# Hybrid pool/mLSTM block on one core: the eight kept weight units of z are loaded raw and split on the chip in every block

## The chip, the cores and the metric

The kernel runs on one core of a Trainium2 chip. The metric is the device time of one execution in microseconds (us), the median of several. In this text TensorE is PE in the profile (PEld its weight loads), VectorE is DVE, ScalarE is ACT, GpSimd is POOL, and SyncE is SP. A row with a q behind the engine (ACTq, SPq) is the issue of a DMA from that engine's queue.

## The reference, cut to what matters

```python
h = rms_norm(x, norm_g) * (1.0 + scale) + shift          # scale, shift, gate from c
proj = h @ w_in                                          # 1024 -> 8 groups of 512 columns
u, z_pool, q, k, v, o, z_mlstm, gates = split(proj)
pool_out = causal_pool_mixer(u, w_pool, ls_pool) * silu(z_pool)
q, k = silu(causal_depthwise_conv(q and k, conv_w, conv_b))   # 4 taps
hm = mlstm_chunkwise(q, k, v, ig, lf)                    # chunks of 128 positions, 4 heads
mlstm_out = norm(hm) * mh_norm_g * sigmoid(o) * silu(z_mlstm)
x = x + gate * (concat(pool_out, mlstm_out) @ w_out)
return rms_norm(x, final_g)
```

x is 1 x 4096 x 1024 in float32. All of it is computed to float32 accuracy.

## The kernel before

**Split operands.** A float32 product is made as three passes: both operands are split into a high part (rounded to the matmul's format) and a low part (the rest), and PE adds high times high, low times high and high times low. For a weight this split costs two instructions on 128 x 512 values: an ACT copy that writes the high part, and a subtraction that writes the low part, on POOL or on DVE. In block 0 the kernel splits the weights as they come, and stores most of them split in a DRAM tensor (w_kept); later blocks load high and low parts together from there (512 KB a unit) and need no split.

**Blocks and order of work.** The 4096 tokens go through in 8 blocks of 512. On PE every block but the first runs in this order: v for four chunks; the eight q and k tiles (tile 0 to 7, 24 matmuls of 512 columns each); z and o; then for each of four chunks the scores, a u tile, a z_pool tile, numerators and state update; and last the output projection.

**z and o by seven products.** In the blocks after the first, z_mlstm and o (two 2x2 halves each) are made by seven products in place of eight, in the order of `PRODUCTS = (1, 2, 6, 5, 7, 3, 4)`. Each product reads 4 weight units, so there are 28 units u = 0 to 27, with 6 matmuls of 512 columns each. Products 1 and 2 (units 0 to 7) read columns of z in `w_in`, product 4 columns of o, and the others sums of weights that block 1 leaves in `s_kept`. Before the change units 0 to 7 come split from w_kept (`ZO_KEPT = 8`), and units 8 to 27 come raw (256 KB a unit): ACT makes the high part (`split_zo`, L1128), and the low part is made on DVE for the units in `ZO_DVE` (8, 11, 13, 16, 18, 21, 23, 26; L1879) and on POOL for the other twelve (`ZO_POOL`, L1562).

**Ring.** Weight units live in a ring of 8 slots. SP issues one queue of loads in order; each load first waits until PE has used the unit that was in the slot. Units 0 to 7 of z take the slots of the k tiles' half units. From unit 10 on a keys transfer stands between every two loads (`keep_keys`), which waits for DVE's transposes of k (L2026).

**Beside the k tiles.** For each q or k tile, ACT copies the sum out of PSUM twice (L1396 and, with scale and bias, L1397), DVE runs three taps of the convolution (L2110), ACT takes the tanh (L1407), and DVE multiplies (L2126 or L2131). The four steps of a tile follow one another. Behind tile 5 ACT also computes `inter_exponents` (L1270), behind tile 6 it issues two small DMAs (`keep_rows`, L1274 and L1276), and behind tile 7 begins `zo_late`: there ACT splits unit 8, empties product 1's sums (`zo_hold`, L1323), and goes on with unit 9. Every engine runs its own instructions strictly in order; PE waits for each unit's low part by itself.

In block 1 DVE also has the sums `s_kept` and, behind tiles 3 and 5, part of the low halves of the token sums (`low_t`, L1918).

Of the kernel before, what the change touches and what calls it, by code (L numbers as in the profile page):

```python
# [45 lines left out]
OFF_U, OFF_ZP, OFF_Q, OFF_K, OFF_V, OFF_O, OFF_ZM, OFF_G = (512 * i for i in range(8))  # L46
# [9 lines left out]
QK_END = V_UNITS + 16  # L56
ZO_UNITS = 28
# [13 lines left out]

PRODUCTS = (1, 2, 6, 5, 7, 3, 4)
ZO_ORDER = (0, 3, 2, 1)
ZO_KEPT = 8
ZO_RAW = ZO_UNITS - ZO_KEPT
ZO_DVE = [u for u in range(ZO_KEPT, ZO_UNITS) if u % 5 in (1, 3)]
ZO_POOL = [u for u in range(ZO_KEPT, ZO_UNITS) if u not in ZO_DVE]
SUM_LOADS = {7: 1, 13: 2, 17: 3}
SUM_STORES = {10: 0, 15: 1, 18: 2, 22: 3}
SUMS_KEPT = QK_END + ZO_KEPT - 1  # L80


C_NG, C_C, C_BA, C_CW, C_CB, C_LS, C_MG, C_END = 0, 8, 16, 40, 72, 80, 84, 88
# [62 lines left out]
def build(nc, x, c, norm_g, w_ada, b_ada, w_in, b_gates, conv_w, conv_b, w_pool, ls_pool, mh_norm_g,  # L146
# [6 lines left out]
    with ExitStack() as ctx:  # L153
# [27 lines left out]
        s_kept = nc.dram_tensor("s_kept", [4, P, 2, D], F32, kind="Internal").ap()  # L181
# [244 lines left out]
        def _(sp):  # L426
# [38 lines left out]
            def load_w(b, m):  # L465

                slot_free(b, m)
                s = slot(b, m)
                sp.dma_start(both(w_split[:, s, :], m).bitcast(F32), both(w_kept[kept_at(b, m)], m)).then_inc(w_loaded[s], 16)

            def load_zo(b, u):

                m = QK_END + u
                if u < ZO_KEPT:
                    load_w(b, m)
                    return
                slot_free(b, m)
                product, k = PRODUCTS[u // 4], u % 4
                src = {4: w_in_v[:, 4 + k, OFF_O:OFF_O + 512], 3: s_kept[k][:, 1, 512:1024], 5: s_kept[k][:, 1, 0:512],
                       6: s_kept[k][:, 0, 512:1024], 7: s_kept[k][:, 0, 0:512]}[product]  # L480
                sp.dma_start(w_raw[:, slot(b, m), 512:1024], src).then_inc(w_loaded[slot(b, m)], 16)

# [239 lines left out]
        def _(pe):  # L722
# [67 lines left out]
            def one_block(b, last_block, first=False):  # L790
# [5 lines left out]
                def w_wait(m):  # L796
                    if first and m in RAW_NO:
                        pe.wait_ge(w_lo_done, RAW_NO[m] + 1)
                    else:
                        pe.wait_ge(w_loaded[slot(b, m)], 16 * loads(b, m))  # L800
# [101 lines left out]
                def zo_product(product):  # L902

                    of_t = {4: 3, 5: 0, 6: 1, 7: 2}
                    dst = {1: zo_x, 2: zo_z, 3: zo_w, 4: zo_x, 5: zo_y, 6: zo_x, 7: zo_x}[product]
                    for k in range(4):
                        u = 4 * PRODUCTS.index(product) + k
                        if u < ZO_KEPT:
                            w_wait(QK_END + u)
                        elif u in ZO_DVE:  # L910
                            pe.wait_ge(zo_lo_dve, (b - 1) * len(ZO_DVE) + ZO_DVE.index(u) + 1)
                        else:
                            pe.wait_ge(zo_lo_pool, (b - 1) * len(ZO_POOL) + ZO_POOL.index(u) + 1)
                        s = slot(b, QK_END + u)
                        for j in range(2):
                            if product in of_t:
                                n = of_t[product]
                                st_hi, st_lo = t_split[:, n, 0, j, k, :], t_split[:, n, 1, j, k, :]
                            else:
                                kk, c = (k if product == 1 else 4 + k), (2 + j if product == 3 else j)  # L920
                                st_hi, st_lo = hT_hi[:, kk, chunk(c)], hT_lo[:, kk, chunk(c)]
                            last = split3(dst[j][:, :], st_hi, st_lo, w_hi[:, s, :], w_lo[:, s, :],
                                          k == 0 and product not in (4, 6, 7), k == 3, product in (4, 6, 7))
                            if k == 3:
                                last.then_inc(zo_full, 1)
                            elif j == 1:
                                last.then_inc(zo_used, 1)
# [186 lines left out]
        def _(act):  # L1114
            def split_w(m):

                if m not in RAW_NO:
                    return
                act.wait_ge(w_loaded[slot(0, m)], 16 * loads(0, m))
                hi, lo = halves(m)  # L1120
                act.activation(w_split[:, slot(0, m), hi], w_raw[:, slot(0, m), lo], ACT.Copy).then_inc(w_hi_done, 1)

            def split_zo(b, u):

                m = QK_END + u
                s = slot(b, m)
                act.wait_ge(w_loaded[s], 16 * loads(b, m))
                act.activation(w_split[:, s, 0:512], w_raw[:, s, 512:1024], ACT.Copy).then_inc(zo_hi_done, 1)  # L1128
# [100 lines left out]
            def one_block(b, last_block, first=False):  # L1229
# [99 lines left out]
                def zo_late():  # L1329

                    early, after = [oz[:, j, :] for j in range(2)], [oz[:, 2 + j, :] for j in range(2)]
                    split_zo(b, 8)
                    zo_hold(1, early)
                    exponents()
                    for u in range(9, 14):
# [43 lines left out]
                for t in range(16 if first else 8):  # L1379
# [28 lines left out]
                    else:  # L1408
# [1013 lines left out]
```

## Time and profile before

| | us |
|---|---|
| median of 3 runs | 1754.94 |
| lowest and highest run | 1753.93, 1758.83 |
| profiled execution, its own time | 1755.37 |
| profiled execution, span from first to last instruction | 1753.5 |
| PE busy (share of the span) | 1718.7 (98%) |
| DVE busy | 1262.0 (72%) |
| ACT busy | 709.6 (40%) |
| POOL busy | 308.5 (18%) |

The granted TensorE clock is 0.995 of full speed over the span. A timeline row gives the start, the duration, engine, line and operation, the tiles written and read, and in brackets how long the engine sat idle before it and what ended that. Where the instruction count is more than one (x3), the duration is that of all of them together. Pipelined instructions overlap a little: a following ACT operation starts about 0.1 us before the one ahead has ended by its row.

### The profile page before, as it was taken

Reading aid. Unit: us, or ns where it says so; the run is one execution under the profiler, and the core shown is the slowest. Engines: PE = TensorE matmul, PEld = TensorE weight load, DVE = VectorE, ACT = ScalarE, POOL = GpSimd, SP = SyncE. Lnnn points to the kernel's source line nnn. Section 1 sums busy time; section 2 is a strip of 40 time slices with the busy share of each in tenths; the row PEclk is TensorE's granted clock in tenths of the full one; section 3 lists DMA queues with packets and bytes.
Section 4 is the critical chain, followed back from the end, with each engine's and each line's share of the span. In section 5 each row is a group of like instructions: output and inputs, shape, how many; then the busy total and the mean of one; then the engine's idle time right before and its main releaser. Section 6 shows DMA issues by size and latency. Waiting matters only on the chain.

```text
span 1753.5 us, 25355 instructions
## 1 busy us (share of the span) xinstructions
PE 1718.7 (98%) x8921; PEld 1472.6 (84%) x8921; DVE 1262.0 (72%) x2599; ACT 709.6 (40%) x1636; POOL 308.5 (18%) x265
## 2 busy tenths in 40 slices
PE   5999999999999999999999999999999999999998
PEld 5987879878898888988888888888889888898886
DVE  7785788767876677766876668866787658776683
ACT  4445343353433434334433434435343343433421
POOL 0022222030210303003030211303021030300300
PEclk9899999999999999999999999999999999999999
DMA  9989875989556984669737796468955698456852
GB/s 335 324 296 325 242 190 198 345 212 300 142 188 192 251 270 120 209 200 270 231 103 244 224 282 172 163 205 229 301 142 191 192 249 276 115 211 202 256 162 84
DMA packets 393554, 387.75 MB, mean 221 GB/s; under 512 B 258300, under 2 KB 283860, under 8 KB 392916
## 3 DMA queue, kind: packets, MB, share of 16 engines
q1 hardware_dynamic: 378196, 363.44, 67.9%
q10 hardware_dynamic: 15232, 22.69, 4.2%
q8 instruction: 71, 1.16, 0.3%
q14 instruction: 55, 0.45, 0.1%
HBM read 323.99 MB, written 62.06 MB: 220 GB/s over the span
## 4 chain that ended last, share of the span: by engine, by line
PE 86%; DVE 5%; DMA 4%; ACT 1%; issue 1%; SPq 1%; POOL 0%; ACTq 0%; POOLq 0%; DVEq 0%
PE ps_acc L725 19%; PE ps_acc L727 19%; PE ps_acc L726 18%; PE ps_num L725 4%; PE ps_num L727 4%; PE ps_num L726 4%; PE ps_kv L725 2%; PE ps_kv L726 2%; PE ps_kv L727 2%; PE ps_sco L1027 2%; PE ps_num L1046 1%; PE ps_kv L1052 1%; PE ps_num L1045 1%; PE ps_bro L725 1%; PE ps_bro L727 1%
## 5 line engine op out<-in xcount | busy, mean ns | idle before, releaser
L725 PE MATMUL ps_acc<-sb_hT_hi,sb_w_split 128*128 128x512 f32 x1024 | 406.0, 396 | 1.1 <-DVE sb_w_split L1857 1.0
L727 PE MATMUL ps_acc<-sb_hT_hi,sb_w_split 128*128 128x512 f32 x1024 | 399.5, 390 | 0.0
L726 PE MATMUL ps_acc<-sb_hT_lo,sb_w_split 128*128 128x512 f32 x1024 | 398.6, 389 | 0.0
L727 PEld LDWEIGHTS ps_acc<-sb_hT_hi,sb_w_split 128*128 128x128 f32 x1024 | 192.2, 188 | 41.3
L725 PEld LDWEIGHTS ps_acc<-sb_hT_hi,sb_w_split 128*128 128x128 f32 x1024 | 192.4, 188 | 40.6 <-issue 1.9
L726 PEld LDWEIGHTS ps_acc<-sb_hT_lo,sb_w_split 128*128 128x128 f32 x1024 | 192.6, 188 | 37.6
L1562 POOL TENSOR_TENSOR sb_w_split<-sb_w_raw,sb_w_split 128x512 fp32r<-128x512 f32 x84 | 115.1, 1377 | 565.3 <-ACT sb_w_split L1128 565.2
L1128 ACT ACTIVATE sb_w_split<-sb_w_raw 128x512 fp32r<-128x512 f32 x140 | 86.2, 631 | 80.6 <-DMA sb_w_raw<-s_kept 74.3
L2110 DVE SCALAR_TENSOR_TENSOR sb_acc_cv<-sb_shifted,sb_par,sb_acc_cv 128x512 f32<-128x512 f32 x96 | 73.7, 767 | 53.3 <-ACT sb_acc_cv L1397 50.4
L1879 DVE TENSOR_TENSOR sb_w_split<-sb_w_raw,sb_w_split 128x512 fp32r<-128x512 f32 x56 | 59.6, 1064 | 66.2 <-ACT sb_w_split L1128 65.9
L1573 POOL TENSOR_TENSOR sb_h_rs<-sb_h_var,sb_mhalf 128x4 f32<-128x4 f32 x32 | 32.3, 1010 | 401.4 <-DVE sb_h_var L2202 401.4
L725 PE MATMUL ps_acc<-sb_wo_hi,sb_mixm_hi 128*128 128x512 f32 x256 | 100.6, 393 | 1.3 <-DVE sb_silu_zp L2319 1.3
L725 PE MATMUL ps_acc<-sb_wo_hi,sb_mixp_hi 128*128 128x512 f32 x256 | 101.7, 397 | 0.0
L726 PE MATMUL ps_acc<-sb_wo_lo,sb_mixp_hi 128*128 128x512 f32 x256 | 100.2, 392 | 0.0
L727 PE MATMUL ps_acc<-sb_wo_hi,sb_mixp_lo 128*128 128x512 f32 x256 | 100.2, 391 | 0.0
L727 PE MATMUL ps_acc<-sb_wo_hi,sb_mixm_lo 128*128 128x512 f32 x256 | 99.8, 390 | 0.0
L726 PE MATMUL ps_acc<-sb_wo_lo,sb_mixm_hi 128*128 128x512 f32 x256 | 99.7, 389 | 0.0
L2110 DVE SCALAR_TENSOR_TENSOR sb_hm<-sb_shifted,sb_par,sb_hm 128x512 f32<-128x512 f32 x96 | 73.1, 762 | 25.1 <-ACT sb_hm L1397 21.1
L725 PE MATMUL ps_kv<-sb_w_split,sb_hT_hi 128*128 128x256 f32 x256 | 73.7, 288 | 5.6 <-DVE sb_hT_lo L1748 5.6
L726 PE MATMUL ps_kv<-sb_w_split,sb_hT_hi 128*128 128x256 f32 x256 | 73.0, 285 | 0.0
L727 PE MATMUL ps_kv<-sb_w_split,sb_hT_lo 128*128 128x256 f32 x256 | 72.7, 284 | 0.0
L1442 ACT ACTIVATE sb_tanh<-sb_hm 128x128 bf16<-128x128 f32 x128 | 38.0, 298 | 83.9 <-DVE sb_hm L2184 83.9
(293 smaller groups left out, 3929.7 us busy)
## 6 DMA issues: line engine op xcount, KB each, us to landing
sb_w_split<-w_kept SPq DMA_DIRECT2D x288, 512.0 KB, 4.8
sb_w_split<-w_kept SPq DMA_DIRECT2D x56, 520.0 KB, 4.6
sb_w_raw<-s_kept SPq DMA_DIRECT2D x112, 256.0 KB, 4.2
sb_w_raw<-w_in SPq DMA_DIRECT2D x76, 256.0 KB, 4.7
sb_x_res<-x SPq DMA_DIRECT2D x34, 512.0 KB, 4.7
w_kept<-sb_w_split SPq DMA_DIRECT2D x32, 512.0 KB, 6.3
out<-sb_qT SPq DMA_DIRECT2D x32, 512.0 KB, 2.9
sb_x_in<-x SPq DMA_DIRECT2D x112, 128.0 KB, 3.9
```

Source lines behind the costliest of these rows:

```text
L725: pe.matmul(dst, st_hi, mv_hi, start=start, stop=False, skip_group_check=resumed)
L726: pe.matmul(dst, st_hi, mv_lo, start=False, stop=False, skip_group_check=resumed)
L727: return pe.matmul(dst, st_lo, mv_hi, start=False, stop=stop, skip_group_check=resumed)
L1027: last = pe.matmul(sco[:, chunk(h)], kT[:, j, h, :], qT[:, h, chunk(j)], start=True, stop=True)
L1045: pe.matmul(dst, dmat[:, h, :], v[:, j, h, :], start=True, stop=False)
L1046: last = pe.matmul(dst, q_in[:, h, :], cmem[:, h, :], start=False, stop=True)
L1128: act.activation(w_split[:, s, 0:512], w_raw[:, s, 512:1024], ACT.Copy).then_inc(zo_hi_done, 1)
L1442: last = act.activation(junk[:, chunk(h)], hm[:, h, :], ACT.Square, accum_out=h_sq[:, h:h + 1])
L1562: nc.gpsimd.tensor_tensor(w_split[:, s, 512:1024], w_raw[:, s, 512:1024], w_split[:, s, 0:512].bitcast(F32), ALU.subtract).then_inc(zo_lo_ ...
L1573: nc.gpsimd.tensor_tensor(dst, src, mhalf[:, 0:n], ALU.pow).then_inc(done, 1)
L1879: V.tensor_tensor(w_split[:, s, 512:1024], w_raw[:, s, 512:1024], w_split[:, s, 0:512].bitcast(F32), ALU.subtract).then_inc(zo_lo_dve, 1)
L2110: ins = V.scalar_tensor_tensor(conv[t % 2], sh[:, HALO - 3 + n:HALO - 3 + n + BLK], tap[n], conv[t % 2], ALU.mult, ALU.add)
```

## The change

No unit of z and o is kept split any more: `ZO_KEPT` becomes 0, so that all 28 units are loaded raw in blocks 1 to 7, and block 0 does not store its eight units of z. ACT gets eight more splits in each of the blocks 1 to 7: units 0 and 1 behind the tanh of tile 5, units 2 and 3 behind that of tile 6, units 4 and 5 behind that of tile 7, and 6 and 7 at the head of `zo_late`. POOL gets their eight low halves (`ZO_POOL` has now 20 units); DVE's units stay the same.

```diff
-ZO_KEPT = 8
+ZO_KEPT = 0
 ZO_RAW = ZO_UNITS - ZO_KEPT
-ZO_DVE = [u for u in range(ZO_KEPT, ZO_UNITS) if u % 5 in (1, 3)]
+ZO_DVE = [u for u in range(8, ZO_UNITS) if u % 5 in (1, 3)]
 ZO_POOL = [u for u in range(ZO_KEPT, ZO_UNITS) if u not in ZO_DVE]
-SUMS_KEPT = QK_END + ZO_KEPT - 1
+SUMS_KEPT = QK_END + 7
...
             def load_zo(b, u):
 
                 m = QK_END + u
-                if u < ZO_KEPT:
-                    load_w(b, m)
-                    return
                 slot_free(b, m)
                 product, k = PRODUCTS[u // 4], u % 4
-                src = {4: w_in_v[:, 4 + k, OFF_O:OFF_O + 512], 3: s_kept[k][:, 1, 512:1024], 5: s_kept[k][:, 1, 0:512],
+                src = {1: w_in_v[:, k, OFF_ZM:OFF_ZM + 512], 2: w_in_v[:, 4 + k, OFF_ZM:OFF_ZM + 512],
+                       4: w_in_v[:, 4 + k, OFF_O:OFF_O + 512], 3: s_kept[k][:, 1, 512:1024], 5: s_kept[k][:, 1, 0:512],
...
-                        if u < ZO_KEPT:
-                            w_wait(QK_END + u)
-                        elif u in ZO_DVE:
+                        if u in ZO_DVE:
                             pe.wait_ge(zo_lo_dve, (b - 1) * len(ZO_DVE) + ZO_DVE.index(u) + 1)
...
-                    split_zo(b, 8)
+                    for u in range(6, 9):
+                        split_zo(b, u)
                     zo_hold(1, early)
...
+                    if not first and t >= 5:
+                        split_zo(b, 2 * (t - 5))
+                        split_zo(b, 2 * (t - 5) + 1)
                     if t == 5:
                         inter_exponents()
```

On ACT, these are the instructions of block 1 from just behind the tanh of tile 5 to `zo_late`'s exponents (rows of the changed kernel carry its own line numbers: L1393, L1394 and L1404 are what L1396, L1397 and L1407 were, L1124 is the split). Before:

```order
L1270 ACTIVATE sb_silu_zp<-sb_m_row,sb_mp_col 16x128
L1396 ACTIVATE sb_shifted<-ps_acc 128x512
L1397 ACTIVATE sb_acc_cv<-ps_acc,sb_par 128x512
L1407 ACTIVATE sb_tanh<-sb_acc_cv 128x512
L1274 DMA rows_kept<-sb_m_row 16x128
L1276 DMA rows_kept<-sb_silu_zp 16x128
L1396 ACTIVATE sb_shifted<-ps_acc 128x512
L1397 ACTIVATE sb_hm<-ps_acc,sb_par 128x512
L1407 ACTIVATE sb_tanh<-sb_hm 128x512
L1128 ACTIVATE sb_w_split<-sb_w_raw 128x512
L1323 ACTIVATE sb_oz<-ps_num 128x512 x2
L1288 ACTIVATE sb_expo<-sb_expo 128x48
```

With the change, the same place:

```order
L1124 ACTIVATE sb_w_split<-sb_w_raw 128x512 x2
L1266 ACTIVATE sb_silu_zp<-sb_m_row,sb_mp_col 16x128
L1393 ACTIVATE sb_shifted<-ps_acc 128x512
L1394 ACTIVATE sb_acc_cv<-ps_acc,sb_par 128x512
L1404 ACTIVATE sb_tanh<-sb_acc_cv 128x512
L1124 ACTIVATE sb_w_split<-sb_w_raw 128x512 x2
L1270 DMA rows_kept<-sb_m_row 16x128
L1272 DMA rows_kept<-sb_silu_zp 16x128
L1393 ACTIVATE sb_shifted<-ps_acc 128x512
L1394 ACTIVATE sb_hm<-ps_acc,sb_par 128x512
L1404 ACTIVATE sb_tanh<-sb_hm 128x512
L1124 ACTIVATE sb_w_split<-sb_w_raw 128x512 x5
```

Two splits now stand ahead of tile 6's copies, two ahead of the small DMAs and tile 7's copies, and five in place of one behind tile 7's tanh.

On POOL, this is where block 1 begins its work on z. Before, and then with the change:

```order
L1573 TENSOR_TENSOR sb_o_rs<-sb_o_var,sb_mhalf 128x1
L1562 TENSOR_TENSOR sb_w_split<-sb_w_raw,sb_w_split 128x512 x12
L1573 TENSOR_TENSOR sb_h_rs<-sb_h_var,sb_mhalf 128x4 x3
L1573 TENSOR_TENSOR sb_x_rs<-sb_x_var,sb_mhalf 128x4 x2
L1573 TENSOR_TENSOR sb_h_rs<-sb_h_var,sb_mhalf 128x4
```

```order
L1573 TENSOR_TENSOR sb_o_rs<-sb_o_var,sb_mhalf 128x1
L1562 TENSOR_TENSOR sb_w_split<-sb_w_raw,sb_w_split 128x512 x20
L1573 TENSOR_TENSOR sb_h_rs<-sb_h_var,sb_mhalf 128x4 x3
L1573 TENSOR_TENSOR sb_x_rs<-sb_x_var,sb_mhalf 128x4 x2
L1573 TENSOR_TENSOR sb_h_rs<-sb_h_var,sb_mhalf 128x4
```

Twelve low halves have become twenty in each block, with the eight new ones first. On SP's queue, block 2 loads its q, k and first z units. Before, and then with the change:

```order
L469 DMA sb_w_split<-w_kept 128x2x520 x3
L469 DMA sb_w_split<-w_kept 128x1024 x24
L481 DMA sb_w_raw<-s_kept 128x512 x2
L536 DMA keys_kept<-sb_hm 32x16x32
L481 DMA sb_w_raw<-s_kept 128x512
```

```order
L469 DMA sb_w_split<-w_kept 128x2x520 x3
L469 DMA sb_w_split<-w_kept 128x1024 x16
L479 DMA sb_w_raw<-w_in 128x512 x8
L479 DMA sb_w_raw<-s_kept 128x512 x2
L534 DMA keys_kept<-sb_hm 32x16x32
```

The eight loads stand at the same places of the queue, with half the bytes and another source.

## Rows read from the trace of the kernel before

**Rows 1.** Waits of PE from 300 us on, in total, times, longest.

```profile
PE ps_num L725 <- DVE sb_w_split L1879: 1.7, 1, 1.7
```

**Rows 2.** PE timeline: block 4, first matmuls of products 1 and 6.

```profile
982.08 0.39 PE L725 MATMUL ps_num<-sb_w_split,sb_hT_hi 128*128 128x512 f32 x1
...
992.96 0.39 PE L725 MATMUL ps_num<-sb_w_split,sb_t_split 128*128 128x512 f32 x1
```

**Rows 3.** ACT timeline, block 4, from tile 5's tanh to unit 9's split.

```profile
975.68 0.63 ACT L1407 ACTIVATE sb_tanh<-sb_hm 128x512 f32<-128x512 f32 x1 [3.14 <-DVE sb_hm L2110]
976.21 0.39 ACT L1270 ACTIVATE sb_silu_zp<-sb_m_row,sb_mp_col 16x128 f32<-16x128 f32 x1
...
977.21 0.77 ACT L1397 ACTIVATE sb_acc_cv<-ps_acc,sb_par 128x512 f32<-128x512 f32 x1
980.37 0.63 ACT L1407 ACTIVATE sb_tanh<-sb_acc_cv 128x512 f32<-128x512 f32 x1 [2.39 <-DVE sb_acc_cv L2110]
...
980.74 0.43 ACTq L1276 DMA_DIRECT2D rows_kept<-sb_silu_zp  x1
...
982.77 0.77 ACT L1397 ACTIVATE sb_hm<-ps_acc,sb_par 128x512 f32<-128x512 f32 x1
985.94 0.63 ACT L1407 ACTIVATE sb_tanh<-sb_hm 128x512 f32<-128x512 f32 x1 [2.40 <-DVE sb_hm L2110]
...
988.80 0.64 ACT L1128 ACTIVATE sb_w_split<-sb_w_raw 128x512 fp32r<-128x512 f32 x1
```

**Rows 4.** DVE timeline, block 4: tile 6's taps, unit 8's low half.

```profile
978.01 2.33 DVE L2110 SCALAR_TENSOR_TENSOR sb_acc_cv<-sb_shifted,sb_par,sb_acc_cv 128x512 f32<-128x512 f32 x3 [0.78 <-ACT sb_acc_cv L1397]
...
990.21 1.15 DVE L1879 TENSOR_TENSOR sb_w_split<-sb_w_raw,sb_w_split 128x512 fp32r<-128x512 f32 x1
```

**Rows 5.** POOL timeline, block 4: its first low half, unit 9.

```profile
989.51 1.29 POOL L1562 TENSOR_TENSOR sb_w_split<-sb_w_raw,sb_w_split 128x512 fp32r<-128x512 f32 x1 [69.99 <-ACT sb_w_split L1128]
```

**Rows 6.** POOL and DVE timelines, block 0, taps beside two low halves.

```profile
112.42 3.00 POOL L1556 TENSOR_TENSOR sb_w_split<-sb_w_raw,sb_w_split 128x512 fp32r<-128x512 f32 x2 [80.29 <-DVE sb_w_split L1857]
...
112.94 3.81 DVE L2110 SCALAR_TENSOR_TENSOR sb_acc_cv<-sb_shifted,sb_par,sb_acc_cv 128x512 f32<-128x512 f32 x3 [0.58 <-ACT sb_acc_cv L1397]
```

**Rows 7.** Block 1: ACT's three tanhs of tiles 5 to 7, DVE's token halves.

```profile
351.28 0.63 ACT L1407 ACTIVATE sb_tanh<-sb_hm 128x512 f32<-128x512 f32 x1 [4.67 <-DVE sb_hm L2110]
...
357.84 0.63 ACT L1407 ACTIVATE sb_tanh<-sb_acc_cv 128x512 f32<-128x512 f32 x1 [4.49 <-DVE sb_acc_cv L2110]
...
362.43 0.63 ACT L1407 ACTIVATE sb_tanh<-sb_hm 128x512 f32<-128x512 f32 x1 [2.39 <-DVE sb_hm L2110]
...
352.68 2.50 DVE L1918 TENSOR_TENSOR sb_t_split<-sb_t_raw,sb_t_split 128x512 fp32r<-128x512 f32 x4
```

**Rows 8.** PE timeline, block 1: first matmuls of products 1, 2 and 6.

```profile
354.26 0.39 PE L725 MATMUL ps_num<-sb_w_split,sb_hT_hi 128*128 128x512 f32 x1
...
360.13 0.47 PE L725 MATMUL ps_acc<-sb_w_split,sb_hT_hi 128*128 128x512 f32 x1 [0.27 <-issue]
...
367.49 0.47 PE L725 MATMUL ps_num<-sb_w_split,sb_t_split 128*128 128x512 f32 x1 [1.65 <-DVE sb_w_split L1879]
```

**Rows 9.** SP timeline, block 4: loads of units 4 to 7.

```profile
973.98 8.61 SPq L469 DMA_DIRECT2D sb_w_split<-w_kept  x4
```

**Rows 10.** The page's DMA issues: KB each, median us from issue to landing.

```profile
sb_w_split<-w_kept SPq DMA_DIRECT2D x288, 512.0 KB, 4.8
```

**Rows 11.** PE timeline, block 0, two matmuls behind an idle stretch.

```profile
254.21 0.49 PE L734 MATMUL ps_bro<-sb_x_sq,sb_same_row 128*128 128x4 f32 x2 [2.24 <-ACT sb_tanh L1149]
...
255.56 0.63 PE L727 MATMUL ps_acc<-sb_wo_hi,sb_mixp_lo 128*128 128x512 f32 x1
255.99 0.63 PE L725 MATMUL ps_acc<-sb_wo_hi,sb_mixp_hi 128*128 128x512 f32 x1
```

**Rows 12.** Busy time by window, with granted clock, DMA share and GB/s.

```profile
255.00:260.00 5.00, 5.00 (x17) 3.94 (x17) 2.16 (x6) 3.40 (x12) 4.22 (x4) 0.72 0.92 138
...
140.00:160.00 20.00, 19.26 (x101) 16.07 (x100) 12.52 (x15) 10.93 (x18) 7.64 (x6) 1.00 1.07 367
```

## The prediction, written before the changed kernel was timed

> **What bounds the kernel now.** I read the busy shares first (the table above): PE is busy for 98% of the span, so time can be lost or won only where PE stands. The view of waits says where: from 300 us on, PE waits once for more than 0.3 us, in block 1 [rows 1]. So blocks 2 to 7 are pure PE time, and anything that makes PE wait there adds to the end, once a block. The first matmul of product 1 in block 4 is at 982.08 and that of product 6, 48 matmuls later, at 992.96 [rows 2]: one matmul each 0.227 us, 1.36 us for a unit's six, 5.44 us for a product or a tile. So unit u is due at 982.08 + 1.36 u: unit 2 at 984.80, unit 4 at 987.52, unit 7 at 991.60. DMA is not what PE waits for in these blocks.
>
> The question is thus whether each of units 0 to 7 has its low part when PE gets there. The timeline of ACT in block 4 [rows 3] shows how far ACT's tile chain lies behind PE: tile 7's sums are ready at 982.08, but its tanh only starts at 985.94. The split of unit 4 now stands behind that tanh. I work through block 4 in order.
>
> **The loads: cost nothing.** SP issues the four loads of units 4 to 7 from 973.98 to 982.59 [rows 9], and such a load lands after 4.8 us [rows 10], so unit 4 is there at 979 and unit 7 at about 987, both ahead of their splits below. They have half the bytes now. If this cover went, ACT would stall in order, with all of its chain.
>
> **Two splits behind tile 5.** A 0.63 us activation gives way to the next after 0.53 us (975.68 to 976.21 [rows 3]). Two take 1.06, so `inter_exponents` starts at 977.27, and tile 6's copies 0.3 us later (its 0.39 less the same overlap of 0.1): L1396 at 977.56, L1397 0.49 later at 978.05 instead of 977.21. The taps started 0.80 behind L1397 (978.01 [rows 4]), so at best at 978.85. Meanwhile POOL starts 0.07 us behind a split's end (988.80 + 0.64 to 989.51 [rows 3, 5]): unit 0 from 976.91 to 978.20, unit 1 to 979.49, at 1.29 each.
>
> **POOL and the taps together.** The trace has one place where taps run beside two low halves: the three take 3.81 us instead of 2.33, the two low halves 3.00 instead of 2.58, and they alternate: the first tap waits for the first low half, holds the second up by 0.42, and taps two and three end 1.33 us behind POOL's end [rows 4, 6]. So a DVE operation with two SBUF inputs and such a POOL operation exclude each other. A third tap adds 0.79 (2.33 less one tap's 0.75, halved), so three taps that wait for the end of a low half end 2.12 us after it. Here: 979.49 + 2.12 = 981.6 and tanh 6 there, instead of 980.37, that is 1.2 late. Without the exclusion it would be 978.85 + 2.33 = 981.2. The Trainium skill (SBUF — State Buffer, section "SBUF: two separate sides") calls this pair of ports an exclusive lock, held for the whole instruction by whichever of the two engines starts first. The trace agrees for DVE, which waits out the low half, and differs for POOL, which is held for 0.42 us of a tap's 0.75; by the rule the unit held up at the end below would come 0.3 us later still, 2 us over the run.
>
> **Two splits behind tile 6.** Tanh 6 at 981.6, unit 2's split at 982.15, unit 3's at 982.7. The two small DMAs issue only when unit 3's split has been sent off: they end 0.79 after it (0.37 from tanh 6 to the start of the second, which takes 0.43 [rows 3]), and with 0.1 to spare tile 7's copies start at 983.6 and L1397 at 984.1, instead of 982.77. POOL: unit 2 from 982.85 to 984.15 (due 984.80, in time), unit 3 to 985.45 (due 986.16, in time). The taps could start at 984.9, wait for unit 3's low half, and end at 985.45 + 2.12 = 987.55: tanh 7 there instead of 985.94.
>
> **Behind tile 7: PE waits.** Unit 4's split runs from 988.1 to 988.7, its low half from 988.8 to 990.07. PE was due at 987.52, so it waits **2.55 us**. From there units come each 1.30 us from POOL and go each 1.36 us to PE. DVE's low half of unit 8 (990.21 before [rows 4], 1.6 later now) holds one of them up by 0.42: PE waits about **0.25 us** more, at unit 7. Unit 8 and all behind it are wanted 2.8 us later than before, while their loads are held by the key transposes, which move by only 1.6: no wait more. Sum: **2.8 us a block**, six blocks 2 to 7: 16.8.
>
> **Block 1** is worse, since its tile chain is later: product 1 starts at 354.26 [rows 8] but tanh 5, 6 and 7 are at 351.28, 357.84 and 362.43 [rows 7]. Unit 0's low half fits (352.5 to 353.8). Then POOL and DVE's four token halves (352.68, 2.50 us for four) get into each other: two low halves of 1.29 go between, so DVE is 2.2 us later and tanh 6 is at 360.0. Unit 2's low half then ends at 360.0 + 0.53 + 0.63 + 0.07 + 1.29 = 362.6, due 357.0: PE waits 5.6. Unit 3's ends at 363.9, tanh 7 follows 2.12 later at 366.0, and unit 4's low half ends 2.52 behind it at 368.5; PE, through with unit 3 at 365.3, waits 3.2. Before, product 2 started at 360.13: 8.4 later. Of this the old waits, 1.65 and 0.16 us ahead of units 8 and 10 (the first in [rows 8]), are absorbed, as those units are then long ready; 0.25 for unit 7 comes to it: 6.8.
>
> **TensorE's clock.** The trace shows what idling can cost: PE sat idle for 2.24 us, and then matmuls that take 0.39 us took 0.63, one each 0.43 us instead of 0.23 [rows 11], with a granted clock of 0.72 in that stretch [rows 12]; that is the lower of its two levels, 1.2 GHz, for some eight matmuls, and cost 8 x 0.20 = 1.6 us. Behind the idle 1.65 us in block 1 they had their usual pitch. My 2.55 us lie just above the idling that did it. So I count 1.6 us in four blocks of the six and nothing in the others (bounds 0 and 9.6), and 1 us in block 1: 7.4.
>
> **Block 0** loses eight stores of 512 KB between 119 and 135 us, where the DMA engines have no room (share 1.07 at 140 to 160 [rows 12]). PE idles 0.74 of the 20 us there, so the most that this can give is about 1; I take 0.5.
>
> Sum: 16.8 + 6.8 + 7.4 - 0.5 = 30.5. Added to the profiled execution's own time, 1755.37 (0.4 above the median of the runs), that is 1785.9: **1786 us**.
>
> **Bounds.** Low: no exclusion and no fall of the clock. Tanh 6 at 981.2, tile 7's L1397 at 983.7, tanh 7 at 986.8, unit 4 ready at 989.3: 1.8 a block, 10.8 for six; block 1 has then tanh 6 as before, at 357.84, and unit 4 ready 5.9 later than before, 4 net. 1755.4 + 14.8 = 1770. High: 3.3 a block (POOL held for each tap's whole 0.75), the clock low in each block, 10 for block 1 (6.8 and both its waits with the clock's 1.6): 6 x (3.3 + 1.6) + 10 = 39.4, 1795.
>
> **Rivals.** A: *POOL and DVE hardly meet and the clock holds*: 1770 to 1778. For it: small shifts decide whether a tap asks for the port during a low half. Against it: POOL's two low halves behind tiles 5 and 6 cover 2.6 us in which the taps fall due each time. B: *each stall drops the clock and the loss breeds more*: units 9 and 10 also come late because POOL has 8 more operations of 1.29 us (10.3 a block) at a pace that is PE's own. 1795 to 1805. Against it: POOL is busy for 18% of the span and sat idle before unit 9. C: *no change*: the splits fall into ACT's idle 2.39 us before each tanh, and PE is not touched. It needs unit 4 by 987.52, that is tanh 7 at 985.1 at the latest, when even before the change it was at 985.94. That holds it down. D, on the other side: *the relief of the DMA engines in block 0 decides*: PE is idle for 0.74 of 20 us there [rows 12], and for as much again in the windows around, 3 us at most; if all that goes and the z units are in time, 1752, and 1749 if the old waits of block 1 and its neighbours go too. It decides from the point where tanh 7 comes 0.8 us earlier than in the rows; nothing in the change brings that.
>
> **How the numbers follow.** Forecast (1778 to 1796) 0.62; A 0.15; B 0.11; between C and A (1761 to 1770) 0.05; C 0.04; D 0.03. The range from 1770 to 1797 takes in the forecast and A and leaves out less than 2 in 10. A measurement of this kernel can tell about 0.3% (5 us) from no change: faster 0.03, same 0.05, slower 0.92.
>
> **What the changed profile would show.** PE's first matmul of product 2 waits for POOL's low half, once in each of blocks 2 to 7, about 2.5 us; twice in block 1, 5.6 and 3.2. ACT's tanh 6 comes about 1.2 and tanh 7 about 1.6 us later against product 1's start. Taps that last over 2.33 us stand beside POOL's low halves. Behind some of the waits the matmuls take 0.63 us. I am wrong if no such wait is there, if it is for a DMA, or if time is lost in the out projection or at the u tiles, where I expect everything moved along together.

## The result, and the profile of the changed kernel

The changed kernel took **1787.03 us** (median of 4 runs, 1781.94 to 1788.87) against 1754.43 us for the kernel before in the same session (4 runs, 1753.54 to 1758.83): ratio 1.0176, 95% interval 1.0156 to 1.0197. The profiled execution took 1787.7 us, its span is 1785.9 us, 32.4 more than before.

I read the waits of PE from 300 us on first, since the one row of [rows 1] is what the kernel before had there. The columns are as there: total, times, longest.

```profile
PE ps_acc L723 <- POOL sb_w_split L1562: 18.9, 7, 2.8
PE ps_num L723 <- POOL sb_w_split L1562: 5.3, 1, 5.3
PE ps_bro L1005 <- DVE sb_m_row L2003: 1.5, 1, 1.5
```

The old wait is gone, and GpSimd's low halves are now what PE waits for, eight times. (The third row stands at 345.89, ahead of product 1 of block 1, and e5 below, which has none of the new work, waits 1.46 us there too.) The PE timeline says where: the first matmul of product 2, in block 1 at unit 2 and again at unit 4 (the first two rows), then once in each block. Three of the six blocks stand here, with the first matmul of product 1 of block 4 as the mark that answers to [rows 2].

```profile
359.77 0.80 PE L723 MATMUL ps_num<-sb_w_split,sb_hT_hi 128*128 128x512 f32 x1 [5.27 <-POOL sb_w_split L1562]
366.10 0.66 PE L723 MATMUL ps_acc<-sb_w_split,sb_hT_hi 128*128 128x512 f32 x1 [1.91 <-POOL sb_w_split L1562]
...
578.90 0.47 PE L723 MATMUL ps_acc<-sb_w_split,sb_hT_hi 128*128 128x512 f32 x1 [2.83 <-POOL sb_w_split L1562]
579.21 0.39 PE L724 MATMUL ps_acc<-sb_w_split,sb_hT_hi 128*128 128x512 f32 x1
...
995.85 0.39 PE L723 MATMUL ps_num<-sb_w_split,sb_hT_hi 128*128 128x512 f32 x1
...
1004.29 0.58 PE L723 MATMUL ps_acc<-sb_w_split,sb_hT_hi 128*128 128x512 f32 x1 [2.84 <-POOL sb_w_split L1562]
1004.67 0.63 PE L724 MATMUL ps_acc<-sb_w_split,sb_hT_hi 128*128 128x512 f32 x1
1005.10 0.63 PE L725 MATMUL ps_acc<-sb_w_split,sb_hT_lo 128*128 128x512 f32 x1
...
1217.13 0.47 PE L723 MATMUL ps_acc<-sb_w_split,sb_hT_hi 128*128 128x512 f32 x1 [2.83 <-POOL sb_w_split L1562]
```

Behind the wait at 578.90 the matmuls keep 0.39 us; behind that at 1004.29 they take 0.63, one each 0.43, as in [rows 11]. The windows (busy times as in [rows 12], then granted clock, DMA share, GB/s) show it for blocks 2, 3, 4 and 5: full clock in blocks 2 and 5, lowered in 3 and 4. By the rows of all six blocks the clock is low for 14 matmuls in blocks 3 and 6, for 8 in blocks 4 and 7.

```profile
578.00:582.00 4.00, 3.10 (x14) 2.59 (x15) 3.72 (x5) 3.39 (x8) 4.00 (x4) 1.00 0.59 142
790.00:794.00 4.00, 3.77 (x9) 3.06 (x10) 3.06 (x4) 2.43 (x6) 4.00 (x4) 0.50 0.71 155
1004.00:1008.00 4.00, 3.71 (x9) 2.94 (x10) 3.11 (x4) 3.12 (x7) 4.00 (x4) 0.57 0.73 174
1217.00:1221.00 4.00, 3.87 (x17) 3.23 (x18) 2.98 (x4) 2.97 (x7) 4.00 (x3) 1.00 0.81 181
```

Why POOL is late is seen in block 4. First ACT, which answers to [rows 3]; product 1 starts at 995.85 now, so tile 5's tanh stands 6.40 us ahead of it as before, tile 6's 0.46 ahead (before 1.71) and tile 7's 5.80 behind (before 3.86).

```profile
989.45 0.63 ACT L1404 ACTIVATE sb_tanh<-sb_hm 128x512 f32<-128x512 f32 x1 [3.14 <-DVE sb_hm L2110]
989.99 1.14 ACT L1124 ACTIVATE sb_w_split<-sb_w_raw 128x512 fp32r<-128x512 f32 x2
...
995.39 0.63 ACT L1404 ACTIVATE sb_tanh<-sb_acc_cv 128x512 f32<-128x512 f32 x1 [2.83 <-DVE sb_acc_cv L2110]
...
1001.65 0.63 ACT L1404 ACTIVATE sb_tanh<-sb_hm 128x512 f32<-128x512 f32 x1 [3.43 <-DVE sb_hm L2110]
1002.19 2.69 ACT L1124 ACTIVATE sb_w_split<-sb_w_raw 128x512 fp32r<-128x512 f32 x5
```

Then POOL and DVE in the same stretch (POOL's three rows first), which answer to [rows 4, 5].

```profile
990.69 2.55 POOL L1562 TENSOR_TENSOR sb_w_split<-sb_w_raw,sb_w_split 128x512 fp32r<-128x512 f32 x2 [57.31 <-ACT sb_w_split L1124]
996.62 2.54 POOL L1562 TENSOR_TENSOR sb_w_split<-sb_w_raw,sb_w_split 128x512 fp32r<-128x512 f32 x2 [3.39 <-ACT sb_w_split L1124]
1002.88 9.74 POOL L1562 TENSOR_TENSOR sb_w_split<-sb_w_raw,sb_w_split 128x512 fp32r<-128x512 f32 x7 [3.71 <-ACT sb_w_split L1124]
...
992.60 2.76 DVE L2110 SCALAR_TENSOR_TENSOR sb_acc_cv<-sb_shifted,sb_par,sb_acc_cv 128x512 f32<-128x512 f32 x3 [0.58 <-ACT sb_acc_cv L1394]
...
996.99 0.96 DVE L2014 COPY sb_m_prev<-sb_m_prev 128x4 f32<-128x4 f32 x1
997.98 1.20 DVE L2106 COPY sb_shifted<-sb_halo_qk 128x3 f32<-128x3 f32 x1
999.29 2.33 DVE L2110 SCALAR_TENSOR_TENSOR sb_hm<-sb_shifted,sb_par,sb_hm 128x512 f32<-128x512 f32 x3
```

For comparison, DVE at the same place in the kernel before, where POOL is idle and the taps wait for ACT's copy:

```profile
981.97 0.17 DVE L2014 COPY sb_m_prev<-sb_m_prev 128x4 f32<-128x4 f32 x1
982.18 0.17 DVE L2106 COPY sb_shifted<-sb_halo_qk 128x3 f32<-128x3 f32 x1
983.58 2.33 DVE L2110 SCALAR_TENSOR_TENSOR sb_hm<-sb_shifted,sb_par,sb_hm 128x512 f32<-128x512 f32 x3 [1.23 <-ACT sb_hm L1397]
```

Tile 6's taps last 2.76 us instead of 2.33. Tile 7's last 2.33, but two tiny copies ahead of them, of 4 and 3 elements a partition, take 0.96 and 1.20 us in place of 0.17: each ends within 0.1 us of one of POOL's two low halves (997.9 and 999.16). Unit 4's low half can thus only start behind the split at 1002.19, and PE, due at 1001.3, starts at 1004.29.

**Where the 32.4 us are.** Taken from one block's product 1 to the next one's (block 7: to the end), in both traces: all up to block 1's is 2.7 us shorter, block 1 is 7.6 longer, blocks 2 to 7 are 3.1, 5.7, 4.7, 3.2, 5.9 and 4.7 longer. Blocks 2 and 5, where the clock holds, show the stall alone: 2.83 of wait and 0.3 more: product 2 starts 3.0 us behind its due time and falls back by 0.17 while it runs. Six times 3.15 is 18.9, and the clock has the rest of these blocks, 8.6.

### The profile page after: what moved, and what is told of

Read it like the earlier page. It is cut to its first block, busy times and chain, and to the rows that moved or that the text cites. A ratio compares the mean times of both kernels' runs of the same rounds, so it can differ in the third digit from the quotient of the medians.

```text
span 1785.9 us, 25451 instructions
## 1 busy us (share of the span) xinstructions
PE 1728.4 (97%) x8921; PEld 1477.7 (83%) x8921; DVE 1285.6 (72%) x2599; ACT 738.8 (41%) x1692; POOL 382.1 (21%) x321
## 4 chain that ended last, share of the span: by engine, by line
PE 78%; DVE 11%; ACT 3%; DMA 3%; issue 3%; POOL 1%; SPq 1%; ACTq 0%; DVEq 0%; POOLq 0%
PE ps_acc L723 17%; PE ps_acc L725 17%; PE ps_acc L724 17%; PE ps_num L723 3%; PE ps_num L725 3%; PE ps_num L724 3%; DVE sb_acc_cv L2110 2%; PE ps_kv L723 2%; PE ps_kv L724 2%; DVE sb_hm L2110 2%; PE ps_kv L725 2%; PE ps_sco L1023 2%; PE ps_num L1042 1%; PE ps_kv L1048 1%; PE ps_num L1041 1%
## 5 line engine op out<-in xcount | busy, mean ns | idle before, releaser
L1562 POOL TENSOR_TENSOR sb_w_split<-sb_w_raw,sb_w_split 128x512 fp32r<-128x512 f32 x140 | 188.3, 1364 | 524.5 <-ACT sb_w_split L1124 524.0
L1124 ACT ACTIVATE sb_w_split<-sb_w_raw 128x512 fp32r<-128x512 f32 x196 | 117.6, 626 | 79.5 <-DMA sb_w_raw<-s_kept 73.5
L1573 POOL TENSOR_TENSOR sb_h_rs<-sb_h_var,sb_mhalf 128x4 f32<-128x4 f32 x32 | 32.4, 1012 | 404.8 <-DVE sb_h_var L2202 404.8
```

Of the source, the lines that this page charges most:

```text
L1562: nc.gpsimd.tensor_tensor(w_split[:, s, 512:1024], w_raw[:, s, 512:1024], w_split[:, s, 0:512].bitcast(F32), ALU.subtract).then_inc(zo_lo_ ...
L1573: nc.gpsimd.tensor_tensor(dst, src, mhalf[:, 0:n], ALU.pow).then_inc(done, 1)
```

## Experiments

Each one compares with the kernel before in the same session (medians 1755.23 for e1 to e4, 1754.43 for e5 to e8, 1756.49 for e9 and e10). Counted from product 1 to product 1, block 1 of the kernel before lasts 211.3 us and blocks 2 to 6 last 208.1 to 208.3 each; block 7 ends 147.1 behind its product 1. In the expectations a time with a plus (+ 3.86) counts from the start of the block's product 1. Lines left out of an edit are marked by `...`.

**e1_kept47 and e2_kept03: half of the change each.** e1 loads units 0 to 3 raw, e2 units 4 to 7:

```
-ZO_KEPT = 0
+ZO_HELD = [4, 5, 6, 7]        # e2: [0, 1, 2, 3]
...
+                if u in ZO_HELD:
+                    load_w(b, m)
+                    return
```

> The changed kernel, but units 4 to 7 stay kept split as before (product 2), and only units 0 to 3 (product 1) are raw. Theory of the prediction: ACT's tile chain and the exclusion of POOL and DVE delay tile 7's tanh by the same 1.9 us as in the changed kernel, but nothing that product 2 needs stands behind it, so PE does not wait in blocks 2 to 7; block 1 keeps unit 2's wait of about 5.3 us. 1753 to 1760 us. Rival (the load of raw units, or POOL's and ACT's added work as such, costs in proportion to its amount): half the loss stays, about 1771 us.

Measured: 1763.6 (1760.35 to 1766.11), ratio 1.0047 [1.0032, 1.0063].

> The changed kernel, but units 0 to 3 stay kept split and only units 4 to 7 are raw, so that nothing is added behind tiles 5 and 6. Theory: tile 7's tanh stays at 3.86 us behind product 1's start, unit 4 is then ready 3.86 + 0.53 + 0.63 + 0.07 + 1.29 + 0.05 = 6.43 behind it and due at 5.44, so PE waits 1.0 us in each of blocks 2 to 7, too short for the clock to fall, and about 3 net in block 1: 1760 to 1766 us. Rival (the four splits behind tile 7's tanh are the whole cause): 2.8 us a block as in the changed kernel, over 1775 us.

Measured: 1766.56 (1764.88 to 1768.47), ratio 1.0064 [1.0049, 1.0079]. In e2 unit 4's wait is back, short, and the clock never falls behind it in blocks 2 to 7 (block 4):

```profile
996.70 0.47 PE L727 MATMUL ps_acc<-sb_w_split,sb_hT_hi 128*128 128x512 f32 x1 [0.92 <-POOL sb_w_split L1570]
```

The median is 0.6 us above my range, since block 1 is 5.1 us longer where I had about 3.

In e1 the wait at product 2 is gone in blocks 2 to 7 while tile 7's tanh is still 5.80 behind product 1. The halves cost 8.4 and 11.3 us, together 20, and the whole 32.6. So they are not additive: units 0 to 3 make the tile chain late, units 4 to 7 make PE depend on its end, and the 2.83 us and the clock need both. e1 missed its range by 3.6 us: some 5 us of it are block 1, and blocks 2 to 7 are 0.3 to 1.3 longer, most of them by waits of 0.2 to 0.45 at units behind product 2, which I had not expected.

**e3_gap: the splits where ACT is idle.** ACT makes units 0 to 6 behind each tile's copies, ahead of its tanh, instead of behind it:

```
+                        if not first and t >= 5:
+                            for u in ((0, 1), (2, 3), (4, 5, 6))[t - 5]:
+                                split_zo(b, u)
...
-                    if not first and t >= 5:
-                        split_zo(b, 2 * (t - 5))
-                        split_zo(b, 2 * (t - 5) + 1)
```

> The changed kernel with all 28 units raw, but the splits of units 0, 1 stand between tile 5's copies and its tanh, 2, 3 in the same place of tile 6, and 4, 5, 6 of tile 7, where ACT idles 2.4 us for the taps; 7 and 8 are split behind tile 7's tanh. Theory: the copies are not delayed, unit 4's low half is ready about 4 us behind product 1's start (due 5.44), the taps are still drawn out by POOL to about 3.8 us, which nobody on PE waits for; no wait of PE in blocks 2 to 7, block 1 within 2 us of before: 1750 to 1757 us. Rival (POOL's twenty low halves a block cannot keep up, or the raw loads cost): waits at units 6 to 12, 1765 us or more.

Measured: 1782.94 (1781.81 to 1784.49), ratio 1.0158 [1.0143, 1.0173]. The theory fell. POOL's low halves now start when the taps do (DVE and POOL in block 4):

```profile
991.62 4.15 DVE L2110 SCALAR_TENSOR_TENSOR sb_acc_cv<-sb_shifted,sb_par,sb_acc_cv 128x512 f32<-128x512 f32 x3 [0.54 <-ACT sb_acc_cv L1394]
...
992.19 3.03 POOL L1562 TENSOR_TENSOR sb_w_split<-sb_w_raw,sb_w_split 128x512 fp32r<-128x512 f32 x2 [4.03 <-ACT sb_w_split L1124]
998.87 6.52 POOL L1562 TENSOR_TENSOR sb_w_split<-sb_w_raw,sb_w_split 128x512 fp32r<-128x512 f32 x4 [3.66 <-ACT sb_w_split L1124]
```

Three taps take 4.15 us where they took 2.33, and four low halves 6.52 instead of 5.2: each lets the other's next operation wait. Tile 7's tanh is 8.4 us behind product 1 here (8.1 in the other blocks), and PE pays by small waits all through the z products (blocks of 211.6 to 212.7), with no clock fall in blocks 2 to 7. Nearly the changed kernel's time (4 us less) comes out of another sum.

**e4_dve03: no low half of POOL beside the taps.** DVE itself makes the low halves of units 0 to 3; ACT splits as in the changed kernel:

```
-ZO_DVE = [u for u in range(8, ZO_UNITS) if u % 5 in (1, 3)]
+ZO_DVE = [0, 1, 2, 3] + [u for u in range(8, ZO_UNITS) if u % 5 in (1, 3)]
...
+                        if not first and t in (5, 6):
+                            low_zo(2 * (t - 5))
+                            low_zo(2 * (t - 5) + 1)
```

> The changed kernel, but DVE makes the low halves of units 0 to 3 (behind its multiplication for tiles 5 and 6), so that POOL does not work beside the taps; ACT's splits stay where the change put them. Theory: without the exclusion tile 7's tanh comes about 1 us after that of before, PE waits 1.8 to 2.0 us for unit 4 in place of 2.83, and the clock falls less often: 1770 to 1779 us. Rival (ACT's splits alone delay the chain, the exclusion plays no part): the wait stays 2.8 us and the time at 1785.

Measured: 1770.95 (1769.65 to 1773.04), ratio 1.009 [1.0075, 1.0105]. The wait at product 2 in block 4:

```profile
996.30 0.47 PE L723 MATMUL ps_acc<-sb_w_split,sb_hT_hi 128*128 128x512 f32 x1 [1.66 <-POOL sb_w_split L1562]
```

It is 1.66 in place of 2.84 (I had expected 1.8 to 2.0), tile 7's tanh is 4.62 behind product 1 in place of 5.80, and no clock falls in blocks 2 to 7. So half of the changed kernel's loss goes when the engines don't meet beside the taps, though DVE has four operations more.

**e7_pool_only: POOL beside the taps, and nothing on ACT.**

```
+                if u < 4:
...
+                    pool.wait_ge(tanh_ready, tanh_no(b, 5 + u // 2))
+                    nc.gpsimd.tensor_tensor(w_split[:, s, 512:1024], ...).then_inc(zo_lo_pool, 1)
```

> The kernel before with all eight units kept split and no split added to ACT; GpSimd alone gets four low-half subtractions a block, two behind tanh 5 and two behind tanh 6 (on units 0 to 3, whose low parts come out wrong), for which PE waits as in the changed kernel. ACT's two chains of splits are gone, so what is left of the delay is POOL against DVE. Theory: tanh 7 comes 1.1 to 1.5 us later against product 1 than before (+ 3.86), the copies in front of the convolution take about 1 us instead of 0.17 where POOL works, and PE still waits nowhere in blocks 2 to 7, as unit 4 needs nothing behind tanh 7: blocks of 208.1 to 208.5 us; block 1 waits about 2 to 4 us at unit 2 or 3; 1756 to 1762 us. Rival, the delay is all ACT's: tanh 7 stays at + 3.9 and no operation of DVE gets longer.

Measured, one run: 1769.19. ACT, DVE and POOL in block 6, where product 1 starts at 1409.29:

```profile
1415.07 0.63 ACT L1409 ACTIVATE sb_tanh<-sb_hm 128x512 f32<-128x512 f32 x1 [3.98 <-DVE sb_hm L2119]
1420.55 0.63 ACT L1130 ACTIVATE sb_w_split<-sb_w_raw 128x512 fp32r<-128x512 f32 x1 [2.71 <-DMA sb_w_raw<-s_kept]
...
1410.41 0.94 DVE L2023 COPY sb_m_prev<-sb_m_prev 128x4 f32<-128x4 f32 x1
1411.38 1.22 DVE L2115 COPY sb_shifted<-sb_halo_qk 128x3 f32<-128x3 f32 x1
...
1409.59 2.99 POOL L1566 TENSOR_TENSOR sb_w_split<-sb_w_split 128x512 fp32r<-128x512 f32 x2 [2.93 <-ACT sb_tanh L1409]
```

Tile 7's tanh is 5.78 behind product 1, as in the changed kernel to 0.02 us, without a single split of ACT's in the way. The rival (all ACT's) falls: POOL against DVE is enough for the whole delay. That the sums agree so closely is in part chance. In e7 POOL starts right behind the tanh, 0.30 behind product 1, and takes 2.99 us, since DVE's multiplication (1409.48) holds its first low half up; in the changed kernel it waits for ACT's split, starts at 0.77 and takes 2.54. Both end 3.3 behind product 1, and the copies with them. ACT's four splits with DVE's own low halves make 0.76 (e4); this and POOL's share overlap in the changed kernel and do not add up. The time missed my range by 7 us. In block 1 PE waits 5.29 and 11 matmuls are slow, and the block is 5.0 longer; blocks 2 to 7 are 1.2 to 1.7 longer, since with tile 7 the units behind product 2 are late as well: ACT's split of unit 10, which waits for its load, comes 11.26 behind product 1 where it came 9.38 in block 6 of the kernel before (blocks 2 to 7: 11.1 to 12.8 against 9.3 to 10.3). The changed kernel's PE is itself 2.8 us later there and so doesn't see it.

**e5_nostore: what block 0's stores cost.**

```
-KEPT = [m for m in RAW_UNITS if m not in range(QK_END + ZO_KEPT, TILE_UNITS[0])]
+KEPT = [m for m in RAW_UNITS if m not in range(QK_END, TILE_UNITS[0])]
```

> The kernel before, in which block 0 no longer stores the eight split units of z (4 MB less for the DMA queues of block 0); blocks 1 to 7 load eight other split units of the same size in their place, so products 1 and 2 are worked out with wrong weights. Nothing else moves. Theory: the 2.7 us that the changed kernel won up to product 1 of block 1 come from these stores: product 1 of block 1 starts 1.5 to 4 us earlier than at 354.26, blocks 2 to 7 stay at 208.1 to 208.3 us each, and the time is 1751 to 1754 us. Rival, block 0 has the stores for nothing (my prediction allowed 0.5 us): within 1 us of the kernel before, and product 1 of block 1 at 353.8 to 354.5.

Measured: 1753.93 (1752.01 to 1756.35, 11 runs) against 1754.43 (1751.97 to 1756.86, 15 runs), ratio 0.9995 [0.9986, 1.0004]; product 1 of block 1 at 354.02. The rival holds, to within 1 us. The interval runs from 2.5 us faster to 0.7 us slower, so it cannot tell nothing from 0.5 us; the traces say a little more. First PE's one wait between 140 and 160 us in the kernel before (the 0.74 us of [rows 12]), then that window in e5:

```profile
147.08 0.63 PE L889 MATMUL ps_num<-sb_cst,sb_fg 128*128 128x128 f32 x4 [0.74 <-DMA sb_fg<-w_in]
...
140.00:160.00 20.00, 20.00 (x107) 16.96 (x106) 12.82 (x16) 11.12 (x18) 7.60 (x6) 1.00 0.83 253
```

This wait for a load is also in e10 (0.47 us) and e7 (0.35), which keep all eight stores, and in none of the nine traces with fewer. So 0.35 to 0.74 us of PE's waiting goes with the stores; the interval leaves room for 2.5 us at most.

**e6_gap47 and e8_dve03_gap45: two attempts at a version that keeps the idea.** e6 holds units 0 to 3 split and puts 4 to 6 in tile 7's gap; e8 is e4 with units 4 and 5 there:

```
+                        if not first and t == 7:
+                            for u in (4, 5, 6):      # e8: (4, 5)
+                                split_zo(b, u)
```

> Units 0 to 3 stay kept split; units 4 to 7 load raw. ACT splits 4, 5 and 6 ahead of tile 7's tanh, behind that tile's two copies, and 7 and 8 behind the tanh; their low halves are GpSimd's. Tanh 7 waits for the taps for 2.4 us in the kernel before, and three splits fit there. Theory A: POOL's three low halves and tile 7's three taps take turns, as where splits stood in the gaps of tiles 6 and 7 both (taps 4.15 us for three instead of 2.33); tanh 7 comes at product 1's start + 5.7 instead of + 3.86, but unit 4's low half is ready at about + 4.0, 1.4 us ahead of need, and unit 7's at about + 8.5, ahead of its + 9.5: no wait at product 2, at most 0.3 us behind it for unit 8's DVE half; 1753 to 1760 us, block 1 giving 2 to 4 of it. Theory B: any collision with tile 7's taps makes DVE late for the rest of the block (small waits of 0.1 to 0.8 us at units 5 to 10): blocks of 210 to 211 us, 1766 to 1775 us.

> All units load raw, as in the changed kernel. Low halves of units 0 to 3 on DVE, behind the taps of tiles 5 and 6; units 4 and 5 are split ahead of tile 7's tanh (behind that tile's copies), 6 to 8 behind it, with low halves on GpSimd. Theory: with DVE making units 0 to 3, tanh 7 is at + 4.62; POOL's two low halves against tile 7's taps add 0.7 to 1.3 us, so tanh 7 is at + 5.3 to 6.0 but unit 4 is ready by about + 4.5 and unit 6 by about + 8.3 (due at + 8.16): waits of 0 to 0.5 us a block, blocks of 208.3 to 209 us, block 1 3 to 5 us, 1760 to 1766 us. Rival, the collision breeds as where all splits stood ahead of the tanhs: waits at several units, blocks above 210.5 us, 1772 us or more.

Measured: e6 1765.95 (1762.81 to 1769.27), ratio 1.0065 [1.0049, 1.008]; e8 1769.18 (1767.52 to 1773.77), ratio 1.0087 [1.0071, 1.0102]. Both lie between their two theories, e6 at the very edge of B. e6's first matmul of product 2 waits nowhere in blocks 2 to 7, as meant, and tile 7's tanh is 5.69 behind product 1 (expected 5.7), but blocks last 209.0 to 210.1: taps of 4.16 us in that one tile make the units behind late, as in e7. e8 pays 0.68 at product 2 and 0.3 more behind it, and its tile 7's tanh is 6.43 behind product 1, above the 5.3 to 6.0 that I expected. Neither is better than e2, which has no such trick.

**e9_again: a second trace of the changed kernel.**

> The changed kernel once more, unaltered, for a second trace of the same work. Theory: the spread of its runs (1781.94 to 1788.87) is the clock's. The wait at product 2 is again 2.8 us in each of blocks 2 to 7 and 5.2 and 1.9 in block 1, while the number of blocks in which matmuls take 0.63 us behind it need not be four; each such block costs 1.6 or 2.8 us more. Time 1781 to 1789. Rival, the clock falls in the same four blocks because something in these blocks differs: the same blocks again (3, 4, 6 and 7) with the same cost.

Measured, one run: 1784.87. Three of its rows, in blocks 2, 4 and 7, and that of product 1 of block 1:

```profile
354.97 0.39 PE L723 MATMUL ps_num<-sb_w_split,sb_hT_hi 128*128 128x512 f32 x1
...
580.80 0.47 PE L723 MATMUL ps_acc<-sb_w_split,sb_hT_hi 128*128 128x512 f32 x1 [2.84 <-POOL sb_w_split L1562]
...
1003.37 0.77 PE L723 MATMUL ps_acc<-sb_w_split,sb_hT_hi 128*128 128x512 f32 x1 [2.83 <-POOL sb_w_split L1562]
...
1638.54 0.77 PE L723 MATMUL ps_acc<-sb_w_split,sb_hT_hi 128*128 128x512 f32 x1 [2.83 <-POOL sb_w_split L1562]
```

The waits are the same to 0.01 us in blocks 2 to 7, but the clock falls in blocks 4 and 7 alone (1.2 and 2.7 us). In block 1 the first wait is 5.25 again, the second 1.11 where I had expected 1.9. Product 1 of block 1 starts at 354.97, not at 351.57: most of the 2.7 us that block 0 seemed to win are spread between executions, which agrees with e5. The clock has a part in it: from 0 to 350 us the granted clock is 0.98 on average in the traces of the kernel before and of e9, and 1.00 in the changed kernel's first.

**e10_stall: the stall alone.** The kernel before with one wait on PE:

```
...
                             w_wait(QK_END + u)
+                            if u == 4:
+                                pe.wait_ge(zo_lo_pool, (b - 1) * len(ZO_POOL) + ZO_POOL.index(9) + 1)
```

> The kernel before with all eight units kept split and no work added anywhere; only PE's first matmul of product 2 (unit 4) is made to wait for the low half of unit 9 too, which GpSimd ends 8.4 us behind product 1's start, 2.9 us after unit 4 is due. So PE stands idle as long as in the changed kernel, with no operation of GpSimd beside DVE's taps and no later tanh. Theory: each of blocks 2 to 7 gets 2.9 us longer, plus 1.6 to 2.8 us where the clock falls, as in the changed kernel; tanh 7 stays at + 3.86; block 1 has one such wait (about 4 us, of which its old 1.65 us wait is saved); six blocks 17.5, block 1 about 3, the clock 5 to 14: 1780 to 1789 us. Rival, the idling costs its own length only (what is late behind it catches up, or the slow matmuls in the changed kernel came from its other work): 1771 to 1776 us with matmuls of 0.39 us throughout.

Measured: 1785.44 (1780.66 to 1789.15), ratio 1.0172 [1.0146, 1.0198]. PE at product 2 in blocks 4 and 5:

```profile
1003.79 0.47 PE L725 MATMUL ps_acc<-sb_w_split,sb_hT_hi 128*128 128x512 f32 x1 [2.78 <-POOL sb_w_split L1564]
...
1214.99 0.76 PE L725 MATMUL ps_acc<-sb_w_split,sb_hT_hi 128*128 128x512 f32 x1 [2.85 <-POOL sb_w_split L1564]
1215.55 0.63 PE L726 MATMUL ps_acc<-sb_w_split,sb_hT_hi 128*128 128x512 f32 x1
```

Idling of 2.78 to 3.13 us a block, with no work added, gives blocks of 211.1 to 211.5 and, where the clock falls (block 5 in this trace), 212.7; block 1 waits 6.72 and is 5.3 longer (I had expected about 4 and 3), the changed kernel's 7.6. That is the changed kernel's time, and the changed kernel's block lengths from block 2 on. So there the loss is the idling at product 2 and what the clock makes of it; nothing else in it needs explaining.

The length of the idling alone does not say when the clock falls. Two places in block 0, the first in e6, the second in e4, with their first matmuls of 512 columns:

```profile
253.88 0.39 PE L736 MATMUL ps_bro<-sb_x_sq,sb_same_row 128*128 128x4 f32 x2 [1.78 <-ACT sb_tanh L1153]
...
255.72 0.63 PE L727 MATMUL ps_acc<-sb_wo_hi,sb_mixp_hi 128*128 128x512 f32 x1
...
240.48 0.50 PE L723 MATMUL ps_acc<-sb_wo_hi,sb_mixm_hi 128*128 128x512 f32 x1 [2.83 <-DVE sb_silu_zp L2322]
240.82 0.39 PE L724 MATMUL ps_acc<-sb_wo_lo,sb_mixm_hi 128*128 128x512 f32 x1
```

Behind 1.78 us the clock fell, 13 us after another idle stretch of 1.31; behind 2.83 it held. So that my 2.55 lay above the 2.24 of [rows 11] was no reason for a fall, nor are the 0.92 us of e2 shown to be safe by their length.

## Why the prediction was right, step by step

The forecast was 1786, within 1.1 us of the median. By its own steps:

- **The loads cost nothing**: no wait of PE for a load in blocks 2 to 7. Right.
- **Tile 6 1.2 us late**: 1.25 (1.71 ahead of product 1, now 0.46). The step was a low half's end plus 2.12; POOL's second low half ends at 993.24 and the taps at 995.36, 2.12 behind.
- **Tile 7 1.6 us late**: 1.94, the step that was mis-sized. I let the taps wait for POOL with 2.12 us left to go. In the trace the copy ahead of them waits instead, and three whole taps follow, so they end 2.46 behind POOL (999.16 to 1001.62). The two small DMAs that I put on ACT's path issue ahead of the splits and hold nothing up; that error cost nothing, as in my own sum the taps waited for POOL and not for the copies. The trace of the kernel before had the missing piece, in block 0, where a copy of 4 elements a partition runs beside a low half and ends with it:

```profile
118.39 1.30 DVE L2014 COPY sb_m_prev<-sb_m_prev 128x4 f32<-128x4 f32 x1
...
118.36 1.29 POOL L1556 TENSOR_TENSOR sb_w_split<-sb_w_raw,sb_w_split 128x512 fp32r<-128x512 f32 x1 [2.94 <-ACT sb_w_split L1121]
```

- **PE waits 2.55 us in each of blocks 2 to 7**: 2.83 idle, which is 3.0 behind the due time from which I counted: 0.34 from tile 7's tanh, the rest from the way on to PE (2.64 from that tanh, I had 2.52). The 0.25 for unit 7 was less: PE falls back by 0.17 in all of product 2. Together 3.15 a block where I had 2.8, 18.9 in place of 16.8. Of the 2.83, 0.92 are there with no lateness of tile 7 (e2), and its 1.94 come on top. e7 and e4 show that the exclusion is behind most of this lateness (without it 0.76 remain, e4), e10 that the stall costs this and no more.
- **Block 1**: waits of 5.27 and 1.91 where I had 5.6 and 3.2, and 7.6 with its clock falls where I had 7.8. DVE's four token halves take 4.58 us there, 2.08 more than in [rows 7], against the 2.2 that I took, and unit 2 starts 8.20 us behind product 1 (I had 8.34), unit 4 14.53 (14.24). The second wait is shorter since the clock fell behind the first: six matmuls of 0.63 us bring PE to unit 4 1.4 us later. The term for the clock and that for the wait overlap, which I had added up; that the total still agrees to 0.2 is partly luck.
- **The clock falls in four of six blocks, 1.6 each**: four of six in this trace, two in e9's, one in e10's. Its price is 1.2 to 2.8, as 5 to 14 matmuls are slow: 8.6 in this trace for 6.4 predicted, 3.9 in e9's. The count was a guess that this trace happens to meet; the size is right only as an average.
- **Block 0 gives 0.5**: the wait that goes with the stores is 0.35 to 0.74 (e5), so the size was right. The rest of the 2.7 us in the first trace is spread between executions.

Sum in this trace: 18.9 + 8.6 + 7.6 - 2.7 = 32.4, predicted 30.5. The mechanism stood. The clock's share is 2.2 larger than predicted and block 0 gives 2.2 more, which cancels by chance; what is left is the 2.1 of the waits, less 0.2 in block 1. In e9's trace, with 3.9 for the clock, 6.1 for block 1 and a block 0 that is 0.7 longer, the loss is 29.6; the 30.5 lie between the two. Rival A asked that POOL and DVE hardly meet: they meet in each block. Rival B asked for late units 9 and 10; they are not late here, but e1 and e7 show units behind product 2 late once its wait is gone, unit 10 by its load and not by POOL's pace. So this loss was hidden and not absent. Rival C, no change, falls with the waits. Rival D is settled by e5.

The Trainium skill (SBUF — State Buffer, section "Who interferes with whom") says that a copy, where its operands meet certain conditions, can take the port pair that DVE shares with GpSimd, and that of two such instructions the second is blocked until the first has ended. The copies of 0.96 and 1.20 us agree, down to 3 elements a partition; I had read the rule for the taps alone.

## What to carry to other kernels

Moving work onto an engine that looks 80% idle is priced by who shares a port with it, and by what stands next on the other engine, down to its smallest copy: follow the chain to the engine that bounds the time and ask by how much it already trails (here tile 7's tanh was 3.86 us behind a product whose next unit had 5.44 us). When a wait goes, look for the one it hid: e1, e6 and e7 had no wait at product 2 in blocks 2 to 7 and still lost 8 to 15 us, 2.6 to 5.0 of it in block 1. A saving is worth measuring by itself before anything is paid for it: the eight stores that this change removes were worth 0.35 to 0.74 us by the traces, and no difference that 11 runs of e5 could tell (ratio 0.9995 [0.9986, 1.0004]).

## What the runs showed of the hardware

- A DVE copy of 128x3 or 128x4 elements between places in SBUF (the on-chip memory) waits for the end of GpSimd's subtraction: 0.91 to 1.22 us in place of 0.17, in blocks 1 to 7 of the changed kernel and of e7. DVE's 128x512 transposes, with one input from SBUF, take 0.71 us beside it as without it (block 4, 1003.04 us).
- Where taps and low halves are ready at the same time they take turns, and both pay: three taps 4.15 us (2.33 alone), four low halves 6.52 (5.2 alone) (e3). Shifted so that the taps come behind, they take 2.33 to 2.76, and POOL loses nothing (2.55 for two low halves, changed kernel).
- Behind an idle 0.92 or 1.66 us (e2, e4) TensorE's granted clock stayed at 2.4 GHz in blocks 2 to 7; behind 2.78 to 3.13 us it fell to 1.2 GHz in 4, 2 and 1 of six blocks in three traces, with nearly the same idling each time. In block 0 it fell behind 1.78 us (e6) and held behind 2.83 (e4). What decides between them I have not found.
